# Loads and splits for the gate stage moved ahead of the end of the last hyena item

## The chip, the cores and the metric

The kernel runs on one core of one Trainium2 chip. The metric is the device time of one execution in microseconds, the median of several runs. The core has five engines with queues of their own: TensorE (PE, matmuls), VectorE (DVE), ScalarE (ACT), GpSimd (POOL) and SyncE (SP, which only issues DMAs here). They wait for each other through semaphores; each queue runs strictly in its written order.

## What is computed

A hybrid encoder layer over a prompt of 1024 and a sample of 512 tokens, 1024 channels. After a norm and an input projection it has an attention branch (three groups with dilated windows, whose outputs are combined by their log sum), a Hyena branch (two long convolutions by FFT), gates for both, and an output projection.

```
attn = einsum('gbsh,gbshd->bshd', softmax(stack(lses)), stack(outs))
attn_branch = einsum('bse,ed->bsd', attn * silu(gate_a), w_br_a)
hy_branch   = einsum('bse,ed->bsd', hy * silu(gate_h), w_br_h)
merged = sigmoid(g_a) * attn_branch + sigmoid(g_h) * hy_branch
out = einsum('bsd,de->bse', merged, w_out)
y = x + rms_norm(out, post_g)
```

## The kernel before

The program is written out by hand, engine by engine, over one memory area `mem` that each stage cuts anew. The stages are: norm and projection of the Hyena inputs, attention with the projections of its six half groups, twelve Hyena items, the gate stage, and the output product.

**Weights.** `w_in` comes in blocks of 256 columns, 48 of them with `w_out`'s four. For each block b there is a chain over four engines: `w_load` (SP, 1 MB), `w_max` (VectorE, line 649), `w_allmax` (GpSimd, an all-reduce over partitions, line 656), `w_power` (VectorE, lines 673 to 687), `w_hi` (ScalarE, 16-bit high part, line 668) and `w_low` (VectorE, low part, line 694). `w_split` is power and low part. A gate tile is 24 matmuls of 16-bit parts (line 1008) and waits for `w_lo`. Blocks 0 to 29 are done before; `M0` is block 30, the first of the gate stage. Raw blocks alternate between two areas (`mraw`), split blocks go through three (`mring`).

**The last Hyena item** (index 11). VectorE multiplies the spectra (`product`), GpSimd combines them (`combine_wide`, lines 945 and 946), TensorE turns back in four blocks of two banks (`inverse`, line 1228), ScalarE copies these eight banks out (`inverse_copy`, line 1510), first blocks 0 and 1, then 2 and 3, and VectorE recombines both halves (`recombine`, lines 1909 to 1929, which counts `f_post`). GpSimd stores the result (line 965). The area of the normed input `hn` (from BASE) holds Hyena's butterflies until then; before, SP loads block 30 and everything behind it only when the last item is recombined and stored.

**The gate stage.** `MSEQ` sets TensorE's order and ScalarE's: gate tiles `("ga", j, s)` for the attention gate (four column tiles j, three token spans s; j 0 and 1 are block 30's, 2 and 3 block 31's), `("ma", 0, s)` for the merge gate (block 32), and `("T", x, 0)`, four transposes (line 1300) of attention tile x. For each of twelve tiles of 128 tokens GpSimd loads the three groups (line 984, two buffers: tile t waits for tile t - 2's combination), VectorE makes the weights and the sum (lines 1974 to 2005), with one Exp on ScalarE between (line 1529), and then multiplies the tile before by its gate (`gate`, line 1963). On ScalarE each Silu of a gate tile (line 1544) and each Exp need a table load before them, as they alternate; Exp of tile x + 2 stands at `("T", x, 0)`. Behind the last tile the first branch product follows (line 1277), and the rest of the stage.

## Time and profile before

| | us |
|---|---|
| median of 3 runs | 2977.17 (2975.89 to 2980.17) |
| the profiled execution: time / span | 2972.14 / 2970.3 |
| TensorE busy | 2724.8 (92%) |
| VectorE busy | 1438.0 (48%) |
| ScalarE busy | 814.0 (27%) |
| GpSimd busy | 410.8 (14%) |
| TensorE gate tiles and other split products, line 1008 | 1542.5, mean 343 ns, idle before them 50.8 |
| chain that ended last, TensorE's share | 80% |

All rows count from the start of the span. A row of the timeline merges like instructions in order; in brackets is the engine's idle time before it and what ended that. The span is what the prediction's steps are counted on; the median stands 5 us above the profiled execution.

### The profile page before, as it was taken

To read this page: it belongs to the slowest core of one execution; us is meant where nothing else is said; L and a number is where in the kernel's file an instruction comes from. 1 tells how busy PE (TensorE), PEld (TensorE's weight loads), DVE (VectorE), ACT (ScalarE), POOL (GpSimd) and SP (SyncE) were. 2 spreads that over 40 slices of the span, in tenths; PEclk is the share of its full clock that TensorE was granted. 3 is DMA by queue.
4 is the path that set the end of the run, shared out by engine and by line. 5 is a ranking of instruction groups with operands and counts; after the bars stand their busy time and mean duration, and the time that the engine had idled before them with its cause. 6 is when DMAs were issued, how large, how long until landed. Compare 5 with 4: busy or idle time off the path is not lost.

```text
span 2970.3 us, 33375 instructions
## 1 busy us (share of the span) xinstructions
PE 2724.8 (92%) x13372; PEld 1567.4 (53%) x13372; DVE 1438.0 (48%) x2017; ACT 814.0 (27%) x1672; POOL 410.8 (14%) x501
## 2 busy tenths in 40 slices
PE   5999999999999999788888888799399999999997
PEld 3444444667676666644555554455144444444487
DVE  6444331333333232279999989587482222222253
ACT  5333322343434343412222221122241111100132
POOL 0000000000000000133333334334000000000000
PEclk8999999999999999889999999899699999999999
DMA  6522211010101010211111111210631130000022
GB/s 209 207 82 90 88 72 60 24 51 26 53 26 49 26 51 14 86 62 33 32 61 61 32 36 43 85 50 29 220 113 36 43 128 29 15 29 29 32 90 86
DMA packets 103762, 192.03 MB, mean 65 GB/s; under 512 B 4927, under 2 KB 78887, under 8 KB 103224
## 3 DMA queue, kind: packets, MB, share of 16 engines
q1 hardware_dynamic: 88280, 115.05, 12.3%
q0 software_dynamic: 15184, 68.56, 6.2%
q10 hardware_dynamic: 144, 6.29, 0.6%
q8 instruction: 107, 1.75, 0.3%
q14 instruction: 47, 0.39, 0.0%
HBM read 141.55 MB, written 54.62 MB: 66 GB/s over the span
## 4 chain that ended last, share of the span: by engine, by line
PE 80%; DVE 11%; issue 5%; DMA 2%; ACT 1%; SPq 0%; POOL 0%; DVEq 0%; ACTq 0%; POOLq 0%
PE ps L1008 49%; PE ps L1175 11%; PE ps L1277 8%; DVE mem L1835 4%; PE ps L1228 4%; PE ps L1137 3%; PE ps L1109 2%; PE ps L1122 2%; DVE mem L1738 2%; PE ps L1170 1%; DMA mem<-c_dec 1%; DVE mem L1774 1%; DVE mem L1777 0%; DVE mem L1606 0%; DVE mem L1773 0%
## 5 line engine op out<-in xcount | busy, mean ns | idle before, releaser
L1008 PE MATMUL ps<-mem 128*128 128x512 f16 (+1 forms) x8448 | 1542.5, 343 | 50.8 <-DVE mem L694 36.9
L1008 PEld LDWEIGHTS ps<-mem 128*128 128x128 f16 x8448 | 842.3, 102 | 711.9 <-issue 71.7
L1175 PE MATMUL ps<-mem 128*128 128x512 f32 (+1 forms) x1104 | 460.6, 575 | 40.7 <-DVE mem L1780 39.5
L1175 PEld LDWEIGHTS ps<-mem 128*128 128x128 f32 x1104 | 224.1, 207 | 271.2 <-issue 258.7
L1704 DVE TENSOR_TENSOR mem<-ps,mem 128x512 f32<-128x512 f32 (+2 forms) x144 | 79.8, 554 | 436.8 <-PE ps L1109 407.8
L1277 PE MATMUL ps<-mem 128*128 128x512 f32 x576 | 249.9, 593 | 0.9 <-DVE mem L1963 0.9
L1439 ACT ACTIVATE mem<-ps 128x512 f32<-128x512 f32 (+1 forms) x144 | 72.4, 503 | 411.0 <-PE ps L1122 411.0
L1277 PEld LDWEIGHTS ps<-mem 128*128 128x128 f32 x576 | 109.6, 190 | 133.1 <-issue 129.9
L668 ACT ACTIVATE mem<-mem 128x2048 f16<-128x2048 f32 x48 | 96.0, 2000 | 291.0 <-DVE mem L687 251.2
L694 DVE SCALAR_TENSOR_TENSOR mem<-mem 128x2048 f16<-128x2048 f32 x48 | 112.7, 2349 | 117.4 <-ACT mem L668 117.4
L1228 PE MATMUL ps<-mem 128*128 128x256 f32 x768 | 169.1, 379 | 0.0
L1228 PEld LDWEIGHTS ps<-mem 128*128 128x128 f32 x768 | 145.4, 190 | 19.8 <-issue 1.0
L1559 ACT ACTIVATE mem<-ps,mem 128x512 f32<-128x512 f32 x69 | 47.4, 687 | 381.9 <-PE ps L1008 381.9
L656 POOL PARTITION_ALL_REDUCE mem<-mem x48 | 22.6, 472 | 913.3 <-DVE mem L649 913.3
L1170 PE MATMUL ps<-mem 64*128 64x512 f32 x192 | 63.3, 739 | 81.1 <-DVE mem L1738 62.3
L1681 DVE SCALAR_TENSOR_TENSOR mem<-mem 128x1537 f32<-128x1537 f32 x24 | 43.7, 1819 | 183.1 <-ACT mem L1385 183.1
L1431 ACT ACTIVATE mem<-mem 128x256 f32<-128x256 f32 (+1 forms) x288 | 129.6, 456 | 8.1 <-DVE mem L1710 7.8
L1835 DVE TENSOR_TENSOR mem<-ps,mem 128x1024 f32<-128x1024 f32 x112 | 129.2, 1212 | 0.0
L649 DVE TENSOR_REDUCE mem<-mem 128x1 f32<-128x2048 f32 x48 | 109.3, 2279 | 23.1 <-DMA mem<-in_w_in 23.1
L909 POOL DMA_DIRECT2D s_og<-mem x72 | 39.3, 545 | 563.9 <-ACT mem L1447 563.9
L2044 DVE TENSOR_TENSOR mem<-ps,mem 128x512 f32<-128x512 f32 x24 | 16.6, 692 | 207.0 <-PE ps L1277 167.8
L1137 PE MATMUL ps<-mem 128*128 128x64 f32 x896 | 116.7, 268 | 0.0
(170 smaller groups left out, 2407.1 us busy)
## 6 DMA issues: line engine op xcount, KB each, us to landing
mem<-in_w_in SPq DMA_DIRECT2D x44, 1024.0 KB, 5.1
s_uc<-mem POOLq DMA_DIRECT2D x24, 768.5 KB, 3.9
mem<-s_uc SPq DMA_DIRECT2D x18, 1024.0 KB, 6.5
s_og<-mem POOLq DMA_DIRECT2D x72, 132.0 KB, 2.0
mem<-s_og POOLq DMA_DIRECT2D x12, 792.0 KB, 5.1
mem<-c_dec SPq DMA_DIRECT2D x8, 896.0 KB
s_hn<-mem POOLq DMA_DIRECT2D x1, 6912.0 KB, 19.7
mem<-s_hn SPq DMA_DIRECT2D x3, 2304.0 KB, 19.0
```

Of the source, the lines that this page charges most:

```text
L649: dve.tensor_reduce(amax[b % 3], (raw if b < NB_U + NB_A else mraw)[b % 2].rearrange("p k c -> p (k c)"), AX.X, ALU.max, apply_absolute_va ...
L668: act.activation(w_place(b)[:, 0], (raw if b < NB_U + NB_A else mraw)[b % 2], ACT.Copy, scale=wscale[b % 3]).then_inc(S["w_hi"], 1)
L694: dve.scalar_tensor_tensor(w[:, 1], (raw if b < NB_U + NB_A else mraw)[b % 2], wscale[b % 3], w[:, 0], ALU.mult, ALU.subtract).then_inc(S[ ...
L1008: mm = pe.matmul(out, lhs(a, k), rhs(b, k), start=(k == 0 and x == 0), stop=(k == KD - 1 and x == 2))
L1137: mm = pe.matmul(ps[:, 6 + t % 2, c], pt[N % 2][:, x, P * b:P * b + P], vt[H % 2][:, vi, c], start=(b == 0), stop=(b == len(vs) - 1))
L1170: pe.matmul(ps[:, h, :], h3[r, c:c + P], w4_of(i)[r, 2 * FQ * x:2 * FQ * x + 2 * FQ], start=True, stop=True).then_inc(S["f_gen"], 1)
L1175: mm = pe.matmul(out, ftab[:, P * tab:P * tab + P], a[:, comp, :], start=(x == 0), stop=(x == len(terms) - 1))
L1228: mm = pe.matmul(ps[:, fbank(u), FQ * lane + oc:FQ * lane + oc + w], yf[:, 2 * p + b, FQ * im + c:FQ * im + c + P], itab[:, col:col + w], ...
L1277: mm = pe.matmul(ps[:, n % 8, :], lhs(k), rhs(k), start=(k == 0), stop=(k == kc - 1))
L1431: act.activation(pr[N % 2][:, x, 0:kw], lg[N % 2][:, x, 0:kw], ACT.Exp, bias=o[:, c:c + 1], accum_out=o[:, c + HH:c + HH + 1]).then_inc(S[ ...
L1704: dve.tensor_tensor(l[:, :, c0:c1], ps[:, 2 + N % 2, :].rearrange("p (x c) -> p x c", x=2)[:, :, c0:c1], bias, ALU.add).then_inc(S["a_bias ...
L1835: op = dve.tensor_tensor(o.rearrange("p k a c -> p (k a) c"), z.unsqueeze(1).to_broadcast([P, 4, FQ]), k.rearrange("p k a c -> p (k a) c") ...
```

## The change

It orders the memory of the gate stage so that the areas which are written first lie over areas that Hyena leaves first: `mraw[0]` over the decay table, `mraw[1]` over the transposed signal, `mring[0]` over the signal of even items, `mring[1]` over the transform's tables; `mt`, the attention tiles and `hg` move behind. Block 30 is loaded once the last filter tile is used (`f_gen_used`), block 31 after the last butterfly, `hn` after the last filter transform. VectorE takes maxima of blocks 30 and 31 and splits block 30 between the last item's product and its recombination; ScalarE's `w_hi` of block 30 stands between its copies of inverse blocks 0, 1 and 2, 3; GpSimd's all-reduces of both stand behind its last combination. Block 31 is split right behind the recombination. Attention tiles 0 and 1 are loaded before the last Hyena store. Block 32's split and block 33's maximum move from ahead of the combinations to behind tile 2, block 33's all-reduce to behind the load of tile 2. `MSEQ` starts with six gate tiles, four of block 30.

```diff
--- before.py
+++ after.py
@@ -356,24 +356,25 @@
-        mt = grid(KD, T, BASE + KD * HC)
-        hg = grid(KD, T)
-        ga, at = hg[:, 0:4, :], hg[:, 4:8, :]
-        mraw = [grid(KD, WC) for _ in range(2)]
-        mring = [halves(part(KD * WC), KD, WC) for _ in range(3)]
+        mraw = [grid(KD, WC, BASE + KD * HC), grid(KD, WC)]
+        mring = [halves(part(KD * WC), KD, WC)]
         wb_words = part(KD * WC)
+        mring += [halves(part(KD * WC), KD, WC) for _ in range(2)]
...
         sg = [part(BANK) for _ in range(3)]
         gated = part(BANK)
-        ogt = [mem[:, BASE + KD * HC + i * 6 * OW:BASE + KD * HC + (i + 1) * 6 * OW].rearrange(
-            "p (g a c) -> p g a c", g=3, a=2) for i in range(2)]
-        GSC = BASE + KD * HC + 12 * OW
+        MERGED = top[0]
+        mt = grid(KD, T)
+        OUT = top[0]
+        hg = grid(KD, T)
+        ga, at = hg[:, 0:4, :], hg[:, 4:8, :]
+        ogt = [mem[:, MERGED + i * 6 * OW:MERGED + (i + 1) * 6 * OW].rearrange("p (g a c) -> p g a c", g=3, a=2) for i in range(2)]
+        GSC = MERGED + 12 * OW
...
@@ -557,8 +558,8 @@
-        others = [("ga", j, s) for s in range(1, NSP) for j in range(4)] + [("ma", 0, s) for s in range(NSP)]
-        MSEQ = [("ga", j, 0) for j in range(4)]
+        others = [("ga", j, 1) for j in (2, 3)] + [("ga", j, 2) for j in range(4)] + [("ma", 0, s) for s in range(NSP)]
+        MSEQ = [("ga", j, s) for s in range(2) for j in range(2)] + [("ga", j, 0) for j in (2, 3)]
@@ -797,26 +798,29 @@
                 if i + 1 < NI:
                     load_filter(i + 1)
                     load_signal(i + 1)
+                else:
+                    sp.wait_ge(S["f_gen_used"], GEN0[NI])
+                    w_load(sp, PREPARED)
                 if i >= 1:
                     sp.wait_ge(S["f_post"], 2 * i)
                 c0, nch = chans(i)
                 c0 += KD * (1 + o)
                 sp.dma_start(planes(hx, i), uc_d[c0:c0 + nch, :, UC0[s]:UC0[s] + LENS[s]].rearrange("c p t -> p c t")
                              ).then_inc(S["ld_hx"], 16)
-            for u in range(f_units - 4, f_units):
-                wait_ready(sp, u)
-            sp.wait_ge(S["f_post"], 2 * NI)
-            for sl in range(2):
-                sp.wait_ge(hy_out[sl], 16 * zc_uses(NI - 1))
-            M0 = NB_U + NB_A
-            w_load(sp, M0)
+            M0 = PREPARED
+            sp.wait_ge(S["f_bf"], 3 * NI)
             w_load(sp, M0 + 1)
+            wait_ready(sp, uk[NI - 1][-1])
+            sp.wait_ge(S["f_gen"], GEN0[NI])
             ends = (0, SPANS[1] // 2, COL_S // 2, HC // 2)
             for s in range(NSP):
                 sp.dma_start(hn_words.rearrange("p (k c) -> p k c", k=2 * KD)[:, :, ends[s]:ends[s + 1]],
                              hn_d.rearrange("p (k c) -> p k c", k=2 * KD)[:, :, ends[s]:ends[s + 1]]).then_inc(ld_hm[s], 16)
             w_load(sp, M0 + 2)
             w_load(sp, M0 + 3)
+            sp.wait_ge(S["f_post"], 2 * NI)
+            for sl in range(2):
+                sp.wait_ge(hy_out[sl], 16 * zc_uses(NI - 1))
             ahead = iter(((4, 5, 6), (7,), (8,), (9,), (10, 11, 12, 13, 14), (15,), (16,), (17,)))
             for kind in range(2):
 
@@ -946,6 +950,9 @@
                 nc.gpsimd.tensor_tensor(yf[:, n, FQ:2 * FQ], a[:, FQ:2 * FQ], a[:, 2 * FQ:3 * FQ], ALU.add
                                         ).then_inc(S["f_y"], 1)
 
+            def load_og(t):
+                pool.dma_start(ogt[t % 2], og_d[:, P * t:P * t + P, :, :].rearrange("g p a c -> p g a c")).then_inc(ld_og[t % 2], 16)
+
             for j in range(NTILE):
                 sums(0, j)
             for i in range(NI):
@@ -959,29 +966,27 @@
                     else:
                         combine_long(i, p)
                 s, q, o = ITEMS[i]
+                if i + 1 == NI:
+                    w_allmax(pool, PREPARED)
+                    w_allmax(pool, PREPARED + 1)
                 if o == 1:
                     pool.wait_ge(S["f_post"], 2 * (i + 1))
+                    if i + 1 == NI:
+                        for sl in range(3):
+                            pool.wait_ge(ot_out[sl], 16 * ot_count(6 * NT - 1))
+                        load_og(0)
+                        load_og(1)
                     c, nch = chans(i)
                     pool.dma_start(hy_d[c:c + nch, :, TOK0[s]:TOK0[s] + LENS[s]].rearrange("c p t -> p c t"),
                                    zc_of(i)).then_inc(hy_out[q % 2], 16)
 
             M0 = NB_U + NB_A
-            for b in range(3):
-                w_allmax(pool, M0 + b)
-            for t in range(NT):
-                if t == 0:
+            w_allmax(pool, M0 + 2)
+            for t in range(2, NT):
+                pool.wait_ge(S["g_cmb"], t - 1)
+                load_og(t)
+                if t == 2:
                     w_allmax(pool, M0 + 3)
-                if t == 0:
-                    for u in range(f_units - 4, f_units):
-                        wait_ready(pool, u)
-                    pool.wait_ge(S["f_post"], 2 * NI)
-                    for sl in range(2):
-                        pool.wait_ge(hy_out[sl], 16 * zc_uses(NI - 1))
-                    for sl in range(3):
-                        pool.wait_ge(ot_out[sl], 16 * ot_count(6 * NT - 1))
-                if t >= 2:
-                    pool.wait_ge(S["g_cmb"], t - 1)
-                pool.dma_start(ogt[t % 2], og_d[:, P * t:P * t + P, :, :].rearrange("g p a c -> p g a c")).then_inc(ld_og[t % 2], 16)
             for b in range(4, 9):
                 w_allmax(pool, M0 + b)
             m_all(pool, MT_GH)
@@ -1518,24 +1523,27 @@
                 ahead = K0_UNITS if i + 1 < NI and not wide(i) else 0
                 if ahead:
                     filter_copy(i + 1, range(ahead))
+                if i + 1 == NI:
+                    act.wait_ge(hy_out[0], 16 * zc_uses(NI - 2))
+                    w_hi(act, PREPARED)
                 inverse_copy(i, (2, 3))
                 if i + 1 < NI:
                     filter_copy(i + 1, range(ahead, filter_units(i + 1)))
 
-            act.wait_ge(ld_hm[0], 16)
-
             def combine(t):
                 act.wait_ge(S["g_sc"], 2 * t + 1)
                 act.activation(wts[t % 2][:, 8:32], wts[t % 2][:, 8:32], ACT.Exp).then_inc(S["g_exp"], 1)
 
             M0 = NB_U + NB_A
-            w_hi(act, M0)
+            wait_ready(act, uz[NI - 1][-1])
             w_hi(act, M0 + 1)
-            w_hi(act, M0 + 2)
+            act.wait_ge(S["f_post"], 2 * NI)
             for n, (kind, x, s) in enumerate(MSEQ):
-                if n in (1, 3):
-                    combine(n // 2)
+                if n in (3, 5):
+                    combine(n // 2 - 1)
                 if kind == "T":
+                    if x == 1:
+                        w_hi(act, M0 + 2)
                     if x + 2 < NT:
                         combine(x + 2)
                     continue
@@ -1939,19 +1947,17 @@
                     filter_butterflies(i + 1)
                     dve.wait_ge(S["f_tz"], TR0[i + 2])
                     butterfly(i + 1, 2, tz)
+                M0 = PREPARED
+                if i + 1 == NI:
+                    w_max(dve, M0)
+                    w_max(dve, M0 + 1)
+                    w_split(dve, chain, settle, M0)
                 made = 3 * min(i + 2, NI)
                 recombine(i, 0, made)
                 recombine(i, 1, made)
 
-            M0 = NB_U + NB_A
-            w_max(dve, M0)
-            w_max(dve, M0 + 1)
-            w_split(dve, chain, settle, M0)
             w_split(dve, chain, settle, M0 + 1)
             w_max(dve, M0 + 2)
-            w_split(dve, chain, settle, M0 + 2)
-            w_max(dve, M0 + 3)
-            dve.wait_ge(ld_hm[0], 16)
 
             def gate(t):
 
@@ -2005,6 +2011,9 @@
                 dve.tensor_tensor(acc, acc, tmp, ALU.add).then_inc(S["g_cmb"], 1)
                 if t >= 1:
                     gate(t - 1)
+                if t == 2:
+                    w_split(dve, chain, settle, M0 + 2)
+                    w_max(dve, M0 + 3)
             gate(NT - 1)
             w_split(dve, chain, settle, M0 + 3)
             w_max(dve, M0 + 4)
```

GpSimd at the end of the last item, before (line 946 the last combination, 965 the Hyena store, `ISA` without operands the switch to the all-reduce's code, 656 all-reduces, 984 attention tiles):

```order
L946 TENSOR_TENSOR mem<-mem 128x256
L965 DMA s_hy<-mem 128x4x512
L656 ISA
L656 ISA mem<-mem 128x1 x4
L984 DMA mem<-s_og 128x3x528 x12
L656 ISA mem<-mem 128x1 x5
```

and now (950, 980, 657 and 954 are the same lines):

```order
L950 TENSOR_TENSOR mem<-mem 128x256
L657 ISA
L657 ISA mem<-mem 128x1 x2
L954 DMA mem<-s_og 128x3x528 x2
L980 DMA s_hy<-mem 128x4x512
L657 ISA mem<-mem 128x1
L954 DMA mem<-s_og 128x3x528
L657 ISA mem<-mem 128x1
L954 DMA mem<-s_og 128x3x528 x9
L657 ISA mem<-mem 128x1 x5
```

The switch and two all-reduces have moved ahead of the store, two attention tiles ahead of it too, and the fourth all-reduce now stands between the loads of tiles 2 and 3.

ScalarE at the same place, before (1510 copies of inverse blocks, 668 high parts, 1544 Silu, 1529 Exp):

```order
L1510 ACTIVATE mem<-ps 128x512 x8
L668 ACTIVATE mem<-mem 128x2048 x3
L1544 ACT_TABLE_LOAD
L1544 ACTIVATE mem<-ps,mem 128x512
L1529 ACT_TABLE_LOAD
L1529 ACTIVATE mem<-mem 128x24
L1544 ACT_TABLE_LOAD
```

and now (1515, 669, 1552, 1535):

```order
L1515 ACTIVATE mem<-ps 128x512 x4
L669 ACTIVATE mem<-mem 128x2048
L1515 ACTIVATE mem<-ps 128x512 x4
L669 ACTIVATE mem<-mem 128x2048
L1552 ACT_TABLE_LOAD
L1552 ACTIVATE mem<-ps,mem 128x512 x3
L1535 ACT_TABLE_LOAD
L1535 ACTIVATE mem<-mem 128x24
```

One high part stands amid the eight copies, one before the Silus, and three Silus stand before the first Exp.

TensorE at the end of the transposes, before (1300 transposes, 1008 gate tiles, 1277 branch product):

```order
L1300 MATMUL ps<-mem 128x128 x4
L1008 MATMUL ps<-mem 128x512 x24
L1300 MATMUL ps<-mem 128x128 x4
L1008 MATMUL ps<-mem 128x512 x24
L1300 MATMUL ps<-mem 128x128 x4
L1277 MATMUL ps<-mem 128x512 x12
```

and now (1305, 1013, 1282):

```order
L1305 MATMUL ps<-mem 128x128 x4
L1013 MATMUL ps<-mem 128x512 x24
L1305 MATMUL ps<-mem 128x128 x4
L1013 MATMUL ps<-mem 128x512 x24
L1305 MATMUL ps<-mem 128x128 x12
L1282 MATMUL ps<-mem 128x512 x12
```

The last three tiles' transposes stand without a gate tile between them.

## Rows read from the trace of the kernel before

**Rows 1.** Windows: stretch, length, busy us (instructions) by engine, granted clock, DMA share, GB/s
```profile
2077.00:2114.00 37.00, 0.14 (x1) 0.14 (x2) 18.48 (x31) 2.60 (x2) 1.50 (x3) 0.54 0.61 203
...
2215.00:2500.00 285.00, 285.00 (x1131) 128.26 (x1132) 68.13 (x88) 43.73 (x48) 8.12 (x16) 1.00 0.18 61
```

**Rows 2.** timeline of TensorE: start, us, engine, instructions, idle before and releaser
```profile
1313.18 1.13 PE L1170 MATMUL ps<-mem 64*128 64x512 f32 x4 [0.98 <-DVE mem L1738]
...
1321.95 2.08 PE L1170 MATMUL ps<-mem 64*128 64x512 f32 x4 [4.00 <-DVE mem L1738]
...
2063.00 13.98 PE L1228 MATMUL ps<-mem 128*128 128x256 f32 x64
2113.86 22.55 PE L1008 MATMUL ps<-mem 128*128 128x512 f16 x96 [36.89 <-DVE mem L694]
2148.22 1.11 PE L1300 MATMUL ps<-mem 128*128 128x128 f32 x4 [11.81 <-DVE mem L2005]
...
2155.44 0.60 PE L1300 MATMUL ps<-mem 128*128 128x128 f32 x4
...
2161.05 0.60 PE L1300 MATMUL ps<-mem 128*128 128x128 f32 x4
...
2214.95 7.56 PE L1277 MATMUL ps<-mem 128*128 128x512 f32 x17 [0.88 <-DVE mem L1963]
```

**Rows 3.** timeline of VectorE
```profile
2076.01 0.69 DVE L1909 TENSOR_TENSOR mem<-mem 128x512 f32<-128x512 f32 x1 [10.93 <-ACT mem L1510]
...
2086.92 1.23 DVE L1929 TENSOR_TENSOR mem<-mem 128x1024 f32<-128x1024 f32 x1
...
2129.57 0.15 DVE L673 TENSOR_SCALAR mem<-mem 128x1 int32<-128x1 int32 x1 [0.48 <-POOL mem L656]
...
2134.62 2.28 DVE L649 TENSOR_REDUCE mem<-mem 128x1 f32<-128x2048 f32 x1
2142.74 0.17 DVE L1974 TENSOR_TENSOR mem<-mem 128x8 f32<-128x8 f32 x1 [5.84 <-DMA mem<-s_og]
...
2143.61 0.18 DVE L1980 TENSOR_TENSOR mem<-mem 128x24 f32<-128x24 f32 x1 [0.29 <-ACT mem L1529]
...
2148.08 0.16 DVE L1974 TENSOR_TENSOR mem<-mem 128x8 f32<-128x8 f32 x1
...
2213.21 0.68 DVE L1963 TENSOR_TENSOR mem<-ps,mem 128x512 f32<-128x512 f32 x1
```

**Rows 4.** GpSimd: lines 852 and 656 of the program, and timeline
```profile
L852 POOLq MODIFY_POOL_CONFIG  x2: 11/11/11, 2.4 to 2.4; - x2
...
L656 POOLq MODIFY_POOL_CONFIG  x2: 37/37/37, 2090.6 to 2090.6; - x2
...
6.86 0.34 POOL L852 PARTITION_ALL_REDUCE mem<-mem  x1 [4.49 <-DVE mem L1610]
...
2066.02 0.73 POOL L946 TENSOR_TENSOR mem<-mem 128x256 f32<-128x256 f32 x1
2089.56 0.77 POOL L965 DMA_DIRECT2D s_hy<-mem  x1 [22.82 <-issue]
2102.02 0.38 POOL L656 PARTITION_ALL_REDUCE mem<-mem  x1 [11.69 <-DVE mem L649]
...
2137.83 1.72 POOL L984 DMA_DIRECT2D mem<-s_og  x2 [0.49 <-issue]
```

**Rows 5.** DMA: landing of the normed input; GB/s, 2085 to 2150 us in slices
```profile
DMA to landing us min/median/max: 13.9/19.4/21.1
...
GB/s 0 0 0 149 378 119 103 383 354 347 352 356 357 355 358 354 356 357 353 357 360 359 353 347 350 346 350 59 3 0 0 171 382 184 403 390 114 0 0 26
```

**Rows 6.** timeline of ScalarE
```profile
2077.01 0.60 ACT L1510 ACTIVATE mem<-ps 128x512 f32<-128x512 f32 x1 [1.13 <-PE ps L1228]
...
2132.27 1.28 ACT L1544 ACT_TABLE_LOAD   x1
2133.57 0.69 ACT L1544 ACTIVATE mem<-ps,mem 128x512 f32<-128x512 f32 x1
```

More of the change, by code:

```diff
@@ L375, in build @@
         m16 = halves(mem[:, BASE:BASE + KD * T], KD, T)
-        OUT = BASE + KD * HC + KD * T
         gpost = mem[:, OUT:OUT + D]
```

## Prediction

> **What bounds the kernel now.** I read the busy windows first, then one engine at a time through the seam between the last hyena item and the gate stage. From 2215 us on TensorE is busy all the time; at the seam stands a stretch of 37 us with 0.14 us of matmul [rows 1]. TensorE's timeline gives the hole exactly: the last inverse transform ends at 2063.00 + 13.98 = 2076.98, the first gate matmul starts at 2113.86 after 36.9 us of idle, a second hole of 11.8 us ends at 2148.22, and the first branch product starts at 2214.95 [rows 2]. All matmuls between the first hole and 2214.95 are 15 gate tiles and 12 transposes; one of each takes 5.61 us warm [rows 2], so 15 x 5.18 + 12 x 0.43 = 83 us of work stands in 138 us.
>
> What ends each hole is VectorE's to say. The final recombination ends at 2088.15, block 30's maximum starts only after its load, block 33's maximum starts at 2134.62 and ends 2136.90, and combination tile 0 starts 5.8 us later, on the DMA of its attention tile [rows 3]. GpSimd had started that DMA at 2137.83, straight behind the all-reduce of block 33 [rows 4]. From tile 0 to the end of tile 11 it is VectorE's own chain: (2213.21 - 2148.08) / 11 = 5.92 us per tile, over TensorE's 5.61. So three things end this stage: the late loads, the preparation of four blocks in a row, and a combination chain slower than the matmuls it feeds.
>
> **What the change does, step by step** (times on the clock of the profiled execution).
>
> *Before the recombination.* Block 30 is asked for when the last filter tile is used, some 50 us early, and block 31 and the normed input when TensorE has left the old areas, near 2051. Before, the queue held some 355 GB/s, and the first third of the input landed 13.9 us after its issue [rows 5]. Now the input's 7.1 MB, block 31, the last item's signal and the hyena store are 10 MB, 29 us from 2051: the first third there near 2068, the last near 2081; TensorE wants the first at 2077.8 and the second at 2088. Covered, and if that cover is gone, each us late is a us lost.
> VectorE was idle for 10.93 us up to 2076.01 [rows 3]; two maxima of 2.29 us fit. Then it needs the all-reduce, and here is the one unknown. GpSimd ends its last sum at 2066.75, and must then switch to the all-reduce's code, an instruction of its own (MODIFY_POOL_CONFIG). Before, this stood at 2090.6 and was hidden: the all-reduce at 2102.02 waited for VectorE. So it costs at most 11.4 us there; at the program's start it stands at 2.4 and the all-reduce starts at 6.86, also right behind VectorE, so at most 4.46 us [rows 4]. The lower end is nothing. I take 4.46, the tightest row of the same pair. The Trainium skill (GPSIMD Engine Reference, 2.1 Instruction dispatch) prices the first call of freshly loaded code at about 6 us; the row at the start stays below that. By 6 us the sum below would lose 0.9 us.
> With 4.46 the all-reduce starts at 2066.75 + 0.25 + 4.46 = 2071.5 and ends 2071.85; power, high and low part take 5.1 us (2129.57 to 2134.62 [rows 3]), so block 30 is ready at 2077.0. ScalarE's 2.0 us high part stands ahead of its last four copies, whose last is not ready before 2077.01 [rows 6], and catches up. The recombination waits for VectorE until 2077.1 instead of 2076.01: 1.1 us late. It ends at 2089.2.
> TensorE starts the gate tiles at 2077.8 (last bank copied at 2077.61) in place of 2113.86: 36 us earlier, and warm.
>
> *Behind it.* Block 31's split and block 32's maximum: 5.05 + 2.28, until 2096.6. Attention tiles 0 and 1 go out on GpSimd 1.4 us after the recombination, as the hyena store did at 2089.56 [rows 4], and take about 5 us: there at 2095.6, covered. Tile 0 runs 2096.6 to 2101.9 (5.34 us, 2142.74 to 2148.08 [rows 3]). Tile 1 needs its Exp, which ScalarE issues only behind the Silu of the fifth gate tile: matmuls end at 2077.8 + 5 x 5.18 = 2103.7, Silu 0.69, a table load of 1.28 [rows 6], so Exp at 2105.8, 3.3 us after its scores. From the Exp on a tile takes 4.47 us (2143.61 to 2148.08): tile 1 ends 2110.55. Its gate 0.60, tile 2 5.34, gate 0.60: 2117.1. Now block 32's split and block 33's maximum, moved from ahead of tile 0 to here, same price: 5.05 + 2.28, until 2124.4.
> *The stall moves along.* On GpSimd block 33's all-reduce still stands ahead of a tile's DMA, now that of tile 3. The pair before cost 2142.74 - 2134.62 = 8.12 us from the maximum's start; so tile 3 starts at 2122.15 + 8.12 = 2130.3. It ends 2135.6, and eight more at 5.93 plus 0.4 for the one late DMA end at 2183.5. TensorE meanwhile is ahead (83 us of work from 2077.8 ends at 2161) and waits.
> *The end.* From the last tile to the branch product took 2214.95 - 2213.21 = 1.74 us, so 2185.3 without a clock loss: 29.7 us gained. But only nine gate tiles are left between twelve transposes (eleven before), so the last three transposes stand alone, TensorE idle some 5.5 us between them. Rows show TensorE at its lower clock after 4.00 us of idle: the same four matmuls 2.08 us for 1.13; after the 11.8 us hole a transpose and gate tile took 7.22 us for 5.61 [rows 2]. The branch products started warm before. I take 2.1 us off (0.5 for the transpose at half speed, 1.6 for the restart; ends 0 and 2.5).
> From the branch products on nothing changes: blocks 34 and up are loaded and split where they were.
> Sum: 36.1 for the first hole less 6.4 that comes back as VectorE's chain, less 2.1: **27.6 us**. The profiled execution took 2972.14, 5.0 below the median of 2977.17; taken off the median, **2949.6 us**.
>
> **Rivals.**
> *The switch of GpSimd's code is long* (up to 11.4 us, or slower still beside 355 GB/s of loads). For it: no row bounds it tighter at this place. Against: 4.46 at the start. Then block 30 is ready at 2084, recombination and gate tiles start 6.3 us later than above, TensorE cools: gain 29.7 - 6.3 - 2.1 - 1.7 = 19.6, 2957.6. A late block 31 or a late hyena store, for which ScalarE's high part waits, has the same form.
> *The stall at tile 3 does not come* (the tile's DMA goes out before the all-reduce has to be waited for): then 5.8 more, gain 33.4, 2943.8. Against: the order on GpSimd says otherwise, its queue is strict.
> *ScalarE ties the chain to TensorE: slower.* Exp of tile t stands behind the Silu of the gate tile that follows transpose t - 3, so there is a loop combination, transpose, gate tile, Silu, table, Exp: 0.45 + 5.18 + 0.69 + 1.28 + 0.3 + 4.5 = 12.4 us. Over three tiles it is 4.1 per tile, under 5.93, and hidden. If it closed over one tile, as at the start, ten tiles would cost 6.5 more each: 65 - 29.7 = 35 us slower, 3012. It decides from a distance under 2.1 tiles; before, at this same distance of three, the wait on Exp was 0.3 us (2143.61 [rows 3]), against it.
> *The change does not do what it says:* the waits added for the old areas (recombination done before the first Silu, the store before the high part) take the early start back, and it stands within 0.2%. That needs over 20 us of new waiting ahead of tile 0. Full banks cannot bring it: eight hold 41 us of gate tiles.
>
> **Chances.** Forecast 0.76 (switch between 0 and 6 us), long switch 0.13, no stall 0.05, nothing 0.03, slower 0.03. Runs of this kernel spread by 2 us, and about 0.2% (6 us) is what its measurement tells from no change. Range: from 2944 (no clock loss, no stall, in part) to 2960 (long switch 2957.6 plus the spread). Faster 0.94, same 0.03, slower 0.03.
>
> **What would show it.** TensorE's hole of 36.9 us under 2 us; the first gate matmul near 2078; MODIFY_POOL_CONFIG near 2067 and the all-reduce some 4.5 us behind it; the recombination about 1 us late; a VectorE wait of 3.3 us on Exp in tile 1; a wait of about 5.8 us on the attention tile's DMA at tile 3, not tile 0; the last three transposes at the low clock; the branch product near 2187. The prediction is wrong if the recombination starts past 2080, if tiles 4 to 11 take other than 5.93 us each, or if the stretch behind the first branch product differs from 755.4 us [rows 1, 2].

## Result and profile after

| | before | after |
|---|---|---|
| median, us | 2977.28 (4 runs, 2975.89 to 2980.17) | 2948.70 (4 runs, 2947.24 to 2949.70) |
| ratio, 95% interval | | 0.9902 (0.9885 to 0.9920) |
| profiled execution: time / span | 2972.14 / 2970.3 | 2949.70 / 2947.9 |

The change saves 28.6 us where 27.6 were forecast: 2948.7 beside 2949.6. The two profiled executions are not to be subtracted as wholes, though. The last inverse transform ends at 2076.98 before and at 2081.98 after, though the program up to there is the same for TensorE; over all profiles of this study that point lies between 2076.4 and 2086.2. The difference grows long before anything that the change moves: the same matmul, with 7428 ahead of it, starts at 1302.75 before and at 1306.24 after. I count it as drift; its cause was not looked for. So I read two lengths in each profile. The **seam** runs from the end of the last inverse transform to the first branch product, the **tail** from there to the end of the span. The seam went from 137.97 to 109.08 us, the tail from 755.35 to 756.84: 28.89 gained, 1.49 lost, 27.4 in all. To lay a time of after beside the forecast, subtract 5.0.

Windows of after, the same stretches as [rows 1] moved by 5 us (length, then busy us and instructions of TensorE, its weight load, VectorE, ScalarE, GpSimd, then granted clock, DMA share, GB/s):

```profile
2082.00:2119.00 37.00, 35.37 (x166) 16.34 (x167) 29.62 (x65) 16.34 (x19) 3.59 (x5) 1.00 0.64 214
2220.00:2505.00 285.00, 285.00 (x1159) 128.31 (x1158) 65.43 (x86) 43.47 (x49) 8.25 (x15) 1.00 0.17 58
```

In 37 us in which TensorE had done 0.14 us it now does 35.37, at the full clock. Its timeline in after, answering to [rows 2]:

```profile
2068.00 13.98 PE L1233 MATMUL ps<-mem 128*128 128x256 f32 x64
2083.63 31.24 PE L1013 MATMUL ps<-mem 128*128 128x512 f16 x144 [1.66 <-DVE mem L695]
...
2141.67 1.09 PE L1305 MATMUL ps<-mem 128*128 128x128 f32 x4 [9.94 <-DVE mem L2011]
2142.55 7.11 PE L1013 MATMUL ps<-mem 128*128 128x512 f16 x24
...
2183.17 1.09 PE L1305 MATMUL ps<-mem 128*128 128x128 f32 x4 [4.99 <-DVE mem L2011]
2189.10 1.09 PE L1305 MATMUL ps<-mem 128*128 128x128 f32 x4 [4.84 <-DVE mem L2011]
2191.06 11.96 PE L1282 MATMUL ps<-mem 128*128 128x512 f32 x24 [0.88 <-DVE mem L1969]
```

The hole of 36.9 us is 1.66. Six gate tiles follow in one piece. The transposes that stand alone near 2185 take 1.09 us where [rows 2] show 0.60, and the branch products start slowly: 11.96 us for the first 24. Before, they took 10.57:

```profile
2214.95 10.57 PE L1277 MATMUL ps<-mem 128*128 128x512 f32 x24 [0.88 <-DVE mem L1963]
```

The granted clock in after says the same:

```profile
2183.00:2190.00 7.00, 1.99 (x8) 1.43 (x8) 5.92 (x16) 0.22 (x1) 0.00 (x0) 0.50 0.00 0
2191.00:2203.00 12.00, 11.94 (x25) 5.23 (x26) 6.33 (x9) 2.00 (x1) 0.34 (x1) 0.88 0.27 87
```

0.50 is the low level (1.2 of 2.4 GHz) while TensorE does 1.99 us of work in 7; it is 0.88 on average in the 12 us of the first branch products. VectorE's timeline in after, answering to [rows 3]:

```profile
2070.01 4.47 DVE L650 TENSOR_REDUCE mem<-mem 128x1 f32<-128x2048 f32 x2
2078.29 0.15 DVE L674 TENSOR_SCALAR mem<-mem 128x1 int32<-128x1 int32 x1 [3.81 <-POOL mem L657]
...
2083.40 0.69 DVE L1917 TENSOR_TENSOR mem<-mem 128x512 f32<-128x512 f32 x1
...
2111.99 0.18 DVE L1986 TENSOR_TENSOR mem<-mem 128x24 f32<-128x24 f32 x1 [3.31 <-ACT mem L1535]
...
2136.10 0.17 DVE L1980 TENSOR_TENSOR mem<-mem 128x8 f32<-128x8 f32 x1 [5.79 <-DMA mem<-s_og]
...
2182.94 0.68 DVE L1969 TENSOR_TENSOR mem<-ps,mem 128x512 f32<-128x512 f32 x1
...
2188.87 0.68 DVE L1969 TENSOR_TENSOR mem<-ps,mem 128x512 f32<-128x512 f32 x1
2190.32 0.69 DVE L1969 TENSOR_TENSOR mem<-ps,mem 128x512 f32<-128x512 f32 x1 [0.77 <-PE ps L1305]
```

Both maxima fit into the idle time ahead of the last recombination (2083.40). VectorE stops for 3.81 us on the all-reduce, and the two stops that the forecast sized are there: 3.31 on Exp at tile 1, 5.79 on the attention tile's DMA at tile 3. The gates of the last tiles follow each other by 5.93 us (2182.94, 2188.87); the last one waits 0.77 for the slow transposes. GpSimd in after, answering to [rows 4]: line 657 of the program (durations in ns, first and last start), then the timeline:

```profile
L657 POOLq MODIFY_POOL_CONFIG  x2: 4/4/4, 2072.0 to 2072.0; - x2
```

```profile
2077.88 0.72 POOL L657 PARTITION_ALL_REDUCE mem<-mem  x2 [6.12 <-issue]
...
2130.42 0.34 POOL L657 PARTITION_ALL_REDUCE mem<-mem  x1 [21.18 <-DVE mem L650]
2130.63 1.52 POOL L954 DMA_DIRECT2D mem<-s_og  x2
```

VectorE had block 30's maximum ready by 2072.3, so the 5.9 us from the switch to the all-reduce are the switch's own. And tile 3's DMA goes out at 2130.63, behind block 33's all-reduce, as the strict queue has it. The loads are covered: the parts of the normed input take 17.7 us and more to land (13.9 and more in [rows 5]), but they are issued from 2057 on, and no engine waits for them (landing of the three parts, in after):

```profile
DMA to landing us min/median/max: 17.7/20.0/23.7
```

### The profile page after: what moved, and what is told of

Same layout as the page of the kernel before. It is cut to its first block, busy times and chain, and to the rows that moved or that the text cites. A ratio compares the mean times of both kernels' runs of the same rounds, so it can differ in the third digit from the quotient of the medians.

```text
span 2947.9 us, 33372 instructions
## 1 busy us (share of the span) xinstructions
PE 2728.5 (93%) x13372; PEld 1569.2 (53%) x13372; DVE 1438.0 (49%) x2017; ACT 813.3 (28%) x1672; POOL 410.7 (14%) x501
## 4 chain that ended last, share of the span: by engine, by line
PE 79%; DVE 13%; issue 4%; DMA 2%; ACT 2%; SPq 0%; POOL 0%; DVEq 0%; ACTq 0%; POOLq 0%
PE ps L1013 48%; PE ps L1180 11%; PE ps L1282 8%; DVE mem L1843 4%; PE ps L1233 3%; PE ps L1142 3%; PE ps L1114 2%; PE ps L1127 2%; DVE mem L1746 2%; PE ps L1175 1%; DMA mem<-c_dec 1%; DVE mem L2000 1%; DVE mem L1782 1%; DVE mem L1785 0%; DVE mem L1781 0%
## 5 line engine op out<-in xcount | busy, mean ns | idle before, releaser
L1502 ACT ACTIVATE mem<-ps 128x512 f32<-128x512 f32 x48 | 26.3, 595 | 318.6 <-PE ps L1252 318.5
```

## Experiments

Ten runs, of nine kernels (spread_again is spread once more). The table has for each the start of tile 3's combination and the seam, both from the end of the last inverse transform, the tail, the sum of both against before, and the medians. The sums and the ratios (one less the ratio, times 2977) agree within 2 us but for load_first, whose median falls 2.5 us short of its trace; the runs of one kernel spread by 2.5 to 6.5 us, those of spread by 10.4, so differences of a few us are read from the traces, not from the medians. A trace has its own spread, too: spread and spread_again, two profiles of one kernel, differ by 1.0 us in the seam and 1.2 in the tail. A difference of one or two us between two kernels, read from one trace each, is therefore no more than likely, unless a wait in it accounts for it.

| kernel | tile 3 | seam | tail | sum - before | median | ratio (95%) |
|---|---|---|---|---|---|---|
| before | 83.47 | 137.97 | 755.35 | | 2977.28 | |
| after | 54.12 | 109.08 | 756.84 | -27.4 | 2948.70 | 0.9902 (0.9885 to 0.9920) |
| load_first | 48.21 | 103.44 | 758.50 | -31.4 | 2946.61 | 0.9903 (0.9888 to 0.9918) |
| exp_ahead | 53.40 | 108.32 | 757.39 | -27.6 | 2944.37 | 0.9902 (0.9885 to 0.9918) |
| spread | 56.02 | 111.39 | 756.65 | -25.3 | 2947.46 | 0.9915 (0.9898 to 0.9932) |
| spread_again | 54.01 | 110.35 | 755.50 | -27.5 | 2946.25 | 0.9909 (0.9894 to 0.9924) |
| old_sequence | 52.28 | 106.77 | 755.63 | -30.9 | 2944.41 | 0.9897 (0.9882 to 0.9912) |
| quiet_switch | 62.35 | 117.30 | 758.38 | -17.6 | 2956.08 | one run |
| late_split | 83.84 | 138.78 | 757.65 | +3.1 | 2977.82 | 1.0008 (0.9999 to 1.0018) |
| late_old | 73.26 | 128.28 | 756.76 | -8.3 | 2966.18 | 0.9972 (0.9962 to 0.9982) |
| joined | 46.80 | 101.29 | 756.58 | -35.5 | 2938.29 | 0.9875 (0.9858 to 0.9891) |
| joined_scales | 43.73 | 98.21 | 756.38 | -38.7 | 2934.90 | 0.9865 (0.9850 to 0.9879) |

Each ratio is against runs of before on the same chip (medians there 2973.3 to 2977.3). My theory was the forecast's: the early first gate tile gives the gain, and what is left is VectorE's chain, held up at tile 1 by ScalarE and at tile 3 by GpSimd's queue. The rival: the chain is set elsewhere, and the waits would only move.

### load_first: the stall at tile 3

```diff
                 load_og(t)
-                if t == 2:
+                if t == 3:
                     w_allmax(pool, M0 + 3)
```

> Block 33's all-reduce stands behind the load of attention tile 3 on GpSimd, not behind that of tile 2. The seam is the time from the end of the last inverse transform to the start of the first branch product: 138.0 us before, 109.1 with the change. Theory (VectorE's chain sets the end, and the 5.8 us it waits at tile 3 are in it): the wait goes, the seam is 5.8 us shorter, 103.3, and so is the total, some 2943. Rival (the tile's load is slow for its own sake, or TensorE binds): the wait shrinks by under 2 us or turns up in tiles 4 to 6.

Measured: seam 103.44, 5.64 less; tail 1.66 more, so 4.0 less in all. By the medians alone the kernel can't be told from after (ratio 0.9903 beside 0.9902); the wait itself, and the same step in joined below, carry the reading. GpSimd's timeline in load_first, then VectorE's:

```profile
2113.38 0.76 POOL L954 DMA_DIRECT2D mem<-s_og  x1 [7.59 <-DVE mem L2011]
2126.95 0.34 POOL L657 PARTITION_ALL_REDUCE mem<-mem  x1 [12.82 <-DVE mem L650]
```

```profile
2126.77 0.15 DVE L1980 TENSOR_TENSOR mem<-mem 128x8 f32<-128x8 f32 x1
```

Tile 3's DMA leaves 13.6 us ahead of the all-reduce, and its combination starts at 2126.77 with no wait. But the end has become dearer. TensorE's timeline in load_first:

```profile
2174.11 1.09 PE L1305 MATMUL ps<-mem 128*128 128x128 f32 x4 [5.30 <-DVE mem L2011]
...
2182.00 13.04 PE L1282 MATMUL ps<-mem 128*128 128x512 f32 x24 [0.88 <-DVE mem L1969]
```

The first 24 branch products take 13.04 us, 1.08 more than in after, behind nearly the same idle time (5.30 and 4.84 us, 4.99 and 4.84 in after).

### exp_ahead: the stop on Exp at tile 1

```diff
-                if n in (3, 5):
-                    combine(n // 2 - 1)
+                if n in (3, 4):
+                    combine(n - 3)
```

> The Exp of tile 1 stands on ScalarE ahead of the Silu of the fifth gate tile, not behind it. Theory: the 3.3 us wait of VectorE in tile 1 goes, but the multiplication with the gate of tile 0 then waits for the sixth gate tile and transpose 0, which TensorE ends at 2115.2; it started at 2116.45. So only 0.7 us are gained, and the wait moves behind tile 1 as some 2.5 us. Rival (ScalarE's order alone was at fault): 3.0 us shorter seam.

Measured: 0.76 less in the seam, 0.2 less with the tail. The stop of 3.31 us left Exp, and one of 2.32 stands at the gate of tile 0, which waits for a Silu (VectorE in exp_ahead):

```profile
2103.58 0.18 DVE L1986 TENSOR_TENSOR mem<-mem 128x24 f32<-128x24 f32 x1 [0.29 <-ACT mem L1535]
2110.45 0.69 DVE L1969 TENSOR_TENSOR mem<-ps,mem 128x512 f32<-128x512 f32 x1 [2.32 <-ACT mem L1552]
```

So behind the Exp stands a second limit of nearly the same date, the last gate tile that tile 0 needs; the new order puts it sixth where it was fourth. Moving the Exp alone shifts the wait.

### spread and spread_again: the transposes that stand alone

```diff
-            MSEQ += [("T", x, 0)] + others[x:x + 1]
+            MSEQ += [("T", x, 0)]
+            if x not in (2, 7, 11):
+                MSEQ.append(others[x - (x > 2) - (x > 7)])
```

> The nine gate tiles behind the first transpose are spread so that none stands behind transposes 2 and 7 and one stands ahead of each of the last three. Theory (the last transposes alone let TensorE's clock fall, and that is paid at the last transpose and in the branch products): the seam is 0.5 us shorter, and the stretch from the first branch product to the end 1.5 us shorter (756.8 to 755.4), granted clock 1.0 at the first products; a total 2.0 us lower. Rival (that stretch differs from run to run and the clock costs nothing): under 0.5 us.

Measured: the product block is back at 10.57 us, yet the seam grew by 2.3. This profile was the longest of its four runs, with a first hole of 2.02 us, so I ran the kernel once more.

> The same kernel as spread once more, to see whether its long profiled run was the rule. If the slow start of its gate tiles (32.93 us for six) belonged to a hole of 2.0 us and not to the order of the gate tiles: this profile, if its hole is below 1.7 us, shows the six tiles in 31.2, a wait on Exp of 3.3 and a seam of 107.7. Rival (the order itself costs it): seam near 111 again.

TensorE's timeline in spread:

```profile
2088.17 32.93 PE L1015 MATMUL ps<-mem 128*128 128x512 f16 x144 [2.02 <-DVE mem L697]
...
2178.36 6.64 PE L1015 MATMUL ps<-mem 128*128 128x512 f16 x24
```

and in spread_again:

```profile
2079.69 31.24 PE L1015 MATMUL ps<-mem 128*128 128x512 f16 x144 [1.65 <-DVE mem L697]
...
2167.26 1.09 PE L1307 MATMUL ps<-mem 128*128 128x128 f32 x4 [4.29 <-DVE mem L2013]
2168.14 7.71 PE L1015 MATMUL ps<-mem 128*128 128x512 f16 x24
...
2188.40 10.57 PE L1284 MATMUL ps<-mem 128*128 128x512 f32 x24 [0.88 <-DVE mem L1971]
```

With a hole of 1.65 the six tiles take 31.24 us again, with 2.02 they took 32.93. The hole was longer there because GpSimd's switch took 6.3 us (2076.1 to 2082.42), and behind it the granted clock was low (window of spread):

```profile
2088.17:2091.00 2.83, 2.83 (x9) 1.10 (x10) 2.79 (x6) 0.00 (x0) 0.00 (x0) 0.61 1.09 357
```

In after, the first 2.9 us of gate tiles have 1.00. The seam of spread_again is 110.35, between the two expectations: the tail gives 1.34 back, the seam takes 1.27. VectorE's last gate waits for TensorE's transposes 2.17 us in place of 0.77, since the transposes left alone in mid-stage cost a second slow gate tile (7.71 us for 5.34, behind 4.29 us of idle), and TensorE then ends behind VectorE. Sums: -27.5 against -27.4. Moving the gaps about gained nothing here: what the products no longer lose, a gate tile in mid-stage does.

### old_sequence: was the new order of gate tiles worth having?

The memory, the loads and the early preparation of after, with the tile order and the places of Exp of before:

```diff
-        others = [("ga", j, 1) for j in (2, 3)] + [("ga", j, 2) for j in range(4)] + [("ma", 0, s) for s in range(NSP)]
-        MSEQ = [("ga", j, s) for s in range(2) for j in range(2)] + [("ga", j, 0) for j in (2, 3)]
+        others = [("ga", j, s) for s in range(1, NSP) for j in range(4)] + [("ma", 0, s) for s in range(NSP)]
+        MSEQ = [("ga", j, 0) for j in range(4)]
...
-                if n in (3, 5):
-                    combine(n // 2 - 1)
+                if n in (1, 3):
+                    combine(n // 2)
```

> The new order of the gate tiles is undone: four gate tiles of span 0 first, eleven between the transposes, and the Exps of tiles 0 and 1 where they were; everything else as changed. Theory (VectorE's chain sets the end; the six tiles ahead only bound its start): TensorE waits some 6.6 us for block 31 behind two tiles, transpose 0 is done near 2113.8 in place of 2115.3, Exp 1 does not wait, so the multiplication with gate 0 starts 2.3 us earlier, and the last products start warm: 2.0 more. In all 4.3 us faster than with the change, near 2944.5. Rival (TensorE binds, so its idle time of 6.6 us is lost): 4 to 7 us slower than with the change.

Measured: 2.31 less in the seam, 1.21 less in the tail. TensorE's timeline in old_sequence shows an open hole, for block 31, that does no harm:

```profile
2078.03 10.52 PE L1013 MATMUL ps<-mem 128*128 128x512 f16 x48 [1.63 <-DVE mem L695]
2095.07 12.77 PE L1013 MATMUL ps<-mem 128*128 128x512 f16 x48 [6.53 <-DVE mem L695]
...
2183.17 10.57 PE L1282 MATMUL ps<-mem 128*128 128x512 f32 x24 [0.88 <-DVE mem L1969]
```

TensorE is ahead of VectorE's chain anyway, so its 6.53 us of idle cost nothing. The chain waits 1.91 us for the Exp of tile 1 instead of 3.31 (I had expected no wait), and a gate tile stands before each of the last transposes again. The part of the change that keeps TensorE busy costs 3.5 us by these two traces. By the medians the kernel is the same as after within the intervals. The second pair that differs in this order alone, load_first and joined below, repeats it: 2.15 less in the seam, 1.92 in the tail, ratio 0.9903 to 0.9875.

### quiet_switch: do the loads slow the switch?

```diff
             ends = (0, SPANS[1] // 2, COL_S // 2, HC // 2)
+            sp.wait_ge(S["w_all"], M0 + 2)
             for s in range(NSP):
```

> The loads of the normed input wait until both all-reduces are done, so the DMA engines are idle while GpSimd switches its code. Theory (the switch has its own price of some 5.9 us whatever the queues carry): from MODIFY_POOL_CONFIG to the first all-reduce 5.8 to 5.9 us as with the change, and the first gate matmul waits for the input instead, some 4 us later than with the change. Rival (the code is fetched through engines that the 355 GB/s of loads keep busy): 4.5 us or less, and block 30 is ready 1.4 us earlier.

Line 657 in quiet_switch, its timeline of GpSimd, and the window of the switch:

```profile
L657 POOLq MODIFY_POOL_CONFIG  x2: 8/8/8, 2068.6 to 2068.6; - x2
```

```profile
2074.28 0.72 POOL L657 PARTITION_ALL_REDUCE mem<-mem  x2 [5.88 <-issue]
```

```profile
2068.60:2074.20 5.60, 5.60 (x28) 4.93 (x27) 2.52 (x2) 1.49 (x3) 0.00 (x0) 1.00 0.00 0
```

The same window in after:

```profile
2072.00:2078.00 6.00, 6.00 (x30) 5.28 (x29) 2.48 (x2) 1.45 (x3) 0.12 (x1) 1.00 1.09 356
```

5.7 us with no transfer under way, 5.9 us beside 356 GB/s: the traffic is not the cause. The kernel is 8.2 us longer in the seam for another reason. The input lands at 2084.66, so the first gate tile is 4.4 us later, and block 32, which is loaded behind the input, comes later still (VectorE in quiet_switch):

```profile
2108.25 2.29 DVE L650 TENSOR_REDUCE mem<-mem 128x1 f32<-128x2048 f32 x1 [11.22 <-DMA mem<-in_w_in]
```

Tile 1 no longer waits for its Exp beyond the usual 0.29 us, so it is this block that sets the chain. The early issue of the input and of the blocks behind it is needed.

### late_split and late_old: the early loads alone

late_split keeps the memory and all early loads of after, and puts the maxima, all-reduces, high part and split of block 30 behind the last recombination again:

```diff
                 M0 = PREPARED
-                if i + 1 == NI:
-                    w_max(dve, M0)
-                    w_max(dve, M0 + 1)
-                    w_split(dve, chain, settle, M0)
                 made = 3 * min(i + 2, NI)
                 recombine(i, 0, made)
                 recombine(i, 1, made)
...
+            w_max(dve, M0)
+            w_max(dve, M0 + 1)
+            w_split(dve, chain, settle, M0)
             w_split(dve, chain, settle, M0 + 1)
```

(the same on GpSimd and ScalarE.)

> Loads as early as with the change, but the maxima, all-reduces and the split of block 30 stand behind the last recombination again. Theory (the gain is in doing VectorE's and GpSimd's part inside the last item, the early loads alone bring little): the recombination starts 2.4 us earlier, GpSimd's switch of 5.9 us stands behind the store, TensorE starts some 26 us after the last inverse transform in place of 1.65, the Exp of tile 1, which waits for five gate tiles, comes 25 us later, and the seam is near 134, so the gain over before is 3 to 5 us. Rival (the loads were what was late): the seam within 8 us of the 109.1 with the change.

Measured: no gain, ratio 1.0008; seam 138.78 where I had expected 134. The switch took 8.6 us, not 5.9, the first gate tile came 29.5 us behind the inverse transform, not 26, and the first six took 33.17 us, not 31.24. Where the gain went, by VectorE's waits in late_split from the recombination to the branch product (us in total, times, longest):

```profile
DVE mem L1982 <- ACT mem L1530: 20.4, 12, 12.2
DVE mem L674 <- POOL mem L657: 8.6, 1, 8.6
...
DVE mem L1976 <- DMA mem<-s_og: 5.7, 1, 5.7
```

The gate tiles start 7.35 us sooner than before, but VectorE waits 12.2 us for the first Exp, which now stands behind three Silus, and 5.32 for the second, behind five. With gate tiles that start 30 us late, ScalarE's order is what sets the chain: this is the tie of the forecast's third rival, though not its loop, as from tile 2 on the wait is 0.29. late_old takes that order back as in old_sequence, nothing else:

> late_split (early loads, all preparation behind the recombination) with the order of gate tiles and of Exp of the kernel before. If the new order took back what the early loads gave: late_split's two waits on Exp (12.20 us at tile 0, 5.32 us at tile 1) are each set by the number of gate tiles ahead of the Exp on ScalarE (three and five); with two and four ahead, both Exp come one gate tile (5.2 us) sooner, not two times but once, so the seam falls from 138.8 to about 133.6, and the last gate tiles no longer leave transposes alone: about 132.2, some 6 us below late_split and 5.8 below before; median near 2970, ratio to before 0.998. Rival (late_split lost its gain elsewhere, in contention or in the switch of GpSimd's code): seam stays near 137, ratio 1.000.

VectorE's waits in late_old:

```profile
DVE mem L674 <- POOL mem L657: 8.6, 1, 8.6
DVE mem L1982 <- ACT mem L1530: 7.7, 12, 4.0
...
DVE mem L650 <- DMA mem<-in_w_in: 2.3, 1, 2.3
```

and in before:

```profile
DVE mem L649 <- DMA mem<-in_w_in: 20.2, 3, 11.5
```

Measured: the seam is 10.50 us shorter than late_split's, the total 0.9972 of before. I had counted two and four Silus ahead of the Exps in the old order; they are one and three, so the Exps come two gate tiles (2 x 5.18 = 10.4) sooner, not one. That of tile 1, from which the rest follows, comes 10.4 us sooner, that of tile 0 9.1. The theory holds with the right count, the rival of a loss elsewhere does not.

In the old order of gate tiles, then, the early loads are worth 8 us: VectorE's waits for blocks fall from 20.2 to 2.3 us, but the switch, hidden before, now holds it up for 8.6, and it waits 4.2 us more for Exps. These 8 us are those of all that late_old has of the change; that the attention tiles are loaded ahead of the store, and that block 32 is split behind tile 2, is in them and wasn't tried by itself. The preparation of block 30 (with 31's maximum) ahead of the recombination, added to them, brings 22 more (old_sequence less late_old: 21.5 in the seam).

### joined and joined_scales: what is left

joined is load_first and old_sequence together (two steps, each tried alone above):

> Two steps that ran alone are joined: block 33's all-reduce behind the load of tile 3 (seam 5.6 us shorter, products 1.1 us slower for the clock), and the old order of gate tiles (seam 2.3 shorter, products 1.4 us faster). If they are independent: seam 109.1 - 5.6 - 2.3 = 101.2, the first products at 10.57 us, some 9.4 us less than with the change. Rival (TensorE becomes the bound once the wait at tile 3 is gone, as it idles for block 31): seam 103 or more.

joined_scales further takes the power of blocks 31 and 32 off VectorE's chain, where it had waited 2.2 us for the high part each time, by doing it one step sooner, while other work lies between:

```diff
                     w_split(dve, chain, settle, M0)
+                    w_power(dve, chain, settle, M0 + 1)
...
-            w_split(dve, chain, settle, M0 + 1)
+            w_low(dve, M0 + 1)
...
+                if t == 1:
+                    w_power(dve, chain, settle, M0 + 2)
                 if t == 2:
-                    w_split(dve, chain, settle, M0 + 2)
+                    w_low(dve, M0 + 2)
```

> As joined, and the scales of blocks 31 and 32 are computed a step ahead, so that ScalarE makes the high part while VectorE recombines or combines, and VectorE does not wait 2.2 us for it. Theory (VectorE's chain still sets the end): the first wait of 2.2 us is worth 2.2 through block 31, which the gate tiles of tile 1's Exp wait for, though tile 0 then waits 1.4 us for its attention tile; the second 2.15; seam 101.2 - 4.3 = 96.9. Rival (TensorE or the attention tiles' loads bind): seam over 99.

Measured: joined 101.29 (the gains of 5.6 and 2.3 add up), and beside old_sequence the median falls by 6.1 us. joined_scales 98.21, between its two expectations. VectorE's timeline in joined_scales, then the window of its seam:

```profile
2095.05 2.34 DVE L695 SCALAR_TENSOR_TENSOR mem<-mem 128x2048 f16<-128x2048 f32 x1
...
2101.72 0.17 DVE L1981 TENSOR_TENSOR mem<-mem 128x8 f32<-128x8 f32 x1 [2.13 <-DMA mem<-s_og]
```

```profile
2081.00:2179.00 98.00, 87.22 (x408) 41.27 (x408) 86.93 (x204) 49.79 (x56) 10.66 (x15) 0.97 0.52 166
```

The low part of block 31 comes with no wait, but of the 4.4 us that two such waits gave, 3.1 arrive: tile 0's DMA, started at the recombination's end as before, is now late by 2.13. Tile 0 starts 20.8 us behind the inverse transform in both kernels; most of the gain comes between tiles 2 and 3 (13.19 to 10.40 us). In the 98 us of this seam TensorE is busy for 87.2 and VectorE for 86.9; before it was 87.7 and 92.4 in 138. joined_scales takes 2934.90, ratio 0.9865 to before, and so beats both kernels (after: 0.9902, and the intervals don't meet).

## Why the prediction was right

*The start.* Forecast: TensorE's hole under 2 us, first gate tile at 2077.8. Measured 1.66, and 2083.63 - 5.0 = 2078.6. **The term that was mis-sized** is the switch of GpSimd's code: I took 4.46 us, the bound of the row at the program's start, and it takes 5.9. The recombination started at 2083.40 - 5.0 = 2078.4 instead of 2077.1, 1.3 us late (and short of the 2080 that was to show the prediction wrong), of which 0.8 reached the first gate tile and tile 3. The row at the start bounded another case of the same instruction pair, with other code before it; as a bound for this place it did not hold. The Trainium skill (GPSIMD Engine Reference, 2.1 Instruction dispatch) gives about 6 us for the first call of freshly loaded code. The 5.9 here agrees with that; the 8.6 of late_split and late_old and the at most 4.46 at the program's start do not. A switch of 6 us was to take 0.9 us off the sum, and 0.8 came.

*The chain.* Tile 1 waited 3.31 us for Exp (forecast 3.3), tile 3 5.79 for its DMA (5.8) and started at 2131.1 (2130.3). Tiles 4 to 11 took 5.93 each. The 0.4 us for one late DMA, carried over from before, did not come.

*The end.* Branch product at 2191.06 - 5.0 = 2186.1, where the text's "near 2187" stood; by the sum it was 2185.3 + 0.5 for the transpose, + 0.8 - 0.4 from the two points above. The loss of clock was 0.5 on the transposes and 1.39 on the products, for 0.5 and 1.6. The forecast has the second of these in two places: its sum takes 1.6 off for the slow restart, which falls into the products, but its sign of being wrong asks for an unchanged 755.4 us behind the first product, and "near 2187" puts the loss ahead of it. The stretch took 756.84, 1.49 more. Taken literally, that sign of being wrong came true. The sum's own term, 1.6, was right to 0.2, so it is the sign that contradicts the sum.

*The spread.* The forecast says that runs of this kernel spread by 2 us; its own three span 4.3. The total hit within 0.9 us is luck in part, then: the errors of 0.8, -0.4 and -0.2 us are smaller than the spread, and partly cancel. The mechanism, stop by stop, is not.

*The rivals.* The long switch did not come, though one of 8.6 us exists elsewhere (below). "No stall at tile 3" fell with after and came true in load_first, at the price given: 5.64 for 5.8. ScalarE's loop, the rival on the slower side, did not close in after, but its cost is real: 17.5 us of waiting in late_split. I had asked whether it repeats over all tiles; it strikes at the first two, where three and five Silus stand ahead of an Exp. What saved the change is that its gate tiles start early enough.

*What the forecast did not ask* is which parts of the change work. It took the new order of gate tiles as part of a package; by the traces that costs 3.5 to 4.1 us.

## What to carry over

Work that is moved ahead pays by the chain it feeds: here the preparation of one weight block, with the maximum of the next, in VectorE's idle time brought 22 us, the early loads and what was moved with them 8, and an order that only kept TensorE busy brought a small loss, since TensorE wasn't the bound there. When several engines share one written order, count for each what stands ahead of the first item that the slowest chain needs (three Silus before an Exp, an all-reduce before a tile's DMA): moving one line there gave 5.6 us. And when two profiles of the same code drift apart by several us, measure from a common event, not from the start.

## What the runs showed of the hardware

The switch to the all-reduce's code took 5.7 to 5.9 us behind sums on GpSimd in eight of nine profiles (6.3 in the ninth, spread), whether DMAs moved 0 or 356 GB/s, and 8.6 us in late_split and late_old, where it stood right behind three DMA issues of GpSimd's own, beside 282 GB/s. Line 657 and GpSimd's timeline in late_split:

```profile
L657 POOLq MODIFY_POOL_CONFIG  x2: 37/37/37, 2096.0 to 2096.0; - x2
```

```profile
2094.97 0.77 POOL L977 DMA_DIRECT2D s_hy<-mem  x1
2104.64 0.72 POOL L657 PARTITION_ALL_REDUCE mem<-mem  x2 [8.90 <-issue]
```

Which of the two makes the 2.7 us wasn't tried.

TensorE came through holes of 1.62 to 1.69 us at its full clock (31.24 us for six gate tiles in four profiles, 10.52 for two in three) and started slowly after holes of 2.02, 6.04 and 29.54 us, each seen once with this order: 32.93, 32.95 and 33.17 us for the six, so the shortest cost nearly as much as the longest. The loss at the end of the seam varied between profiles of nearly the same code. The first 24 branch products took 12.49, 12.31, 11.96, 12.97 and 13.04 us where the last transposes but one stood behind 4.46, 4.62, 4.99, 5.30 and 5.30 us of idle and the last behind 4.8, and 10.57 where a gate tile stood between. What decides it wasn't tried.
